# An attention stage whose tiles share a score bank, with two banks of turned tiles and probabilities scaled on GpSimd

## The chip, the cores and the metric

The kernel runs on one core of one Trainium2 chip. The metric is the device time of one execution in microseconds, the median of the runs. Engines are named as in the profile: PE (TensorE matmuls), PEld (its weight loads), DVE (VectorE), ACT (ScalarE), POOL (GpSimd), SP (SyncE).

## The reference

Two transformer layers over 256 context and 1024 latent tokens of width 1024: a gated linear attention layer, then a latent-attention (MLA) layer, each followed by a convolutional feed-forward. The change touches only the attention of the second layer, in fp32:

```
q = rmsnorm((rmsnorm(cq) @ w_uq) per head, q_norm)      # 8 heads, 128 + 64 rotary
k, v = (rmsnorm(ckv) @ w_ukv) per head                  # k_nope 128, v 128
k = rmsnorm(concat(k_nope, k_pe), k_norm)               # over 192
q, k = rope on the last 64
s = q @ k.T * 192 ** -0.5                               # 1024 x 1280 per head
o = softmax(s) @ v
```

## The kernel before

Every fp32 product is made of three passes over fp32r parts: high times high, high times low, low times high. A value is split by copying it to an fp32r tile (its high part, on ACT or POOL) and subtracting that from the original (its low part, on DVE or POOL).

The attention is one stage, with the instruction order of each engine written out by hand. A head has 8 tiles of 128 queries; a tile t has three units, so 24 units a head, numbered 3t + n. For each unit PE, in order: *turns* a part of the probabilities of tile t (`turn_p`, L1633: matmuls against the identity, keys onto partitions, written to PSUM), does any preparation piece due in this unit, then does the third n of the *scores* of tile t+2 (L1621, 12 matmuls of 512 columns and 6 of 256 for a tile). Before an even tile it multiplies the two turned tiles before it with v (`values`, L1644, 30 matmuls of 256 columns). So each engine works two tiles behind the scores.

The others follow: ACT copies the turned part to `pt_hi` (L1738), DVE subtracts to `pt_lo` (L1835). On ACT the exponential of tile t+1 (L1719, which also sums) stands behind the copy of n = 0. On DVE the row maximum of t+1 (L1809, L1814) stands ahead of the subtraction of n = 0; behind that of n = 1 stand the reciprocal of the sum (L1819) and the scaling of the probabilities of t+1 (L1821).

PSUM has 8 banks of 512 columns. Scores of even tiles start at bank 0, those of odd tiles at bank 3, 2.5 banks each; the output of `values` lies in the upper half of bank 2; turned parts have one bank (6), preparation one (7, `work`). With one bank for turned parts, `turn_p` of a unit waits for the subtraction of the unit before:

```
UNITS = ((0, 4), (4, 4), (8, 2))                      # first key tile, key tiles
S_PS, O_PS, T_PS, W_PS = (0, 3 * BANK), 2 * BANK + 256, 6 * BANK, 7 * BANK
pe.wait_ge(ptl_set, h * (QT * NU) + (t * NU + n + 1)) # in turn_p
```

The next head's keys and queries are made in *pieces* between the units, by the table PREPARE: k in three parts with their squares (POOL, L1540), the sums of squares over partitions (k_sum), log and exp for the reciprocal root (ACT, k_log, k_rstd), k_norm (DVE, L1784), the rotary part of k (POOL, L1544, L1547), the high part of k (POOL, L1551), k_low (DVE, L1788), and for each half of the queries q, q_pe (12 matmuls of 512 columns, L1588; q_turn on DVE, L1799), q_pe_low (L1804), q_sum (L1594, 4 products with one column each; two instructions each in the trace, whose squares POOL adds, L1559). All pieces go through the one bank `work`, so each waits for the reader of the one before. The v pieces of the head itself (L1599) are made in units 1 to 3. The head's weights are loaded by SP when all pieces of the head before are done, and split on POOL.

Head 0 is prepared ahead of the loop over the heads, with no tiles beside it. Heads 1 to 6 are a hardware loop of two heads a turn, heads 0 and 7 stand outside it.

Of the kernel before, what the change touches and what calls it, by code (L numbers as in the profile page):

```python
# [26 lines left out]
ALU = mybir.AluOpType  # L27
# [1312 lines left out]
def mla_latents(c, a, raw, cq_hi, cq_lo, ckv, ckv_hi, ckv_lo, k_pe, pe_sq, rope, norms, half):  # L1340
# [16 lines left out]
    with c.stage() as block:  # L1357
# [65 lines left out]
        def _(pool):  # L1423
# [8 lines left out]
PREPARE = {5: (("k", 0),), 7: (("k", 1),), 8: (("k", 2),), 9: (("k_sum", 0),), 10: (("k_sum", 1),),  # L1432
           11: (("k_sum", 2),), 12: (("k_log", 0),), 13: (("k_rstd", 0), ("q", 0)),
           14: (("k_norm", 0), ("q_pe", 0)), 15: (("k_low", 1), ("q_pe_low", 0)), 16: (("k_low", 0), ("q_sum", 0)),
           19: (("q", 1),), 20: (("q_pe", 1),), 21: (("q_pe_low", 1),), 22: (("q_sum", 1),)}

PIECES = (("k", 0), ("k", 1), ("k", 2), ("k_sum", 0), ("k_sum", 1), ("k_sum", 2), ("q", 0), ("q_pe", 0),
          ("q_sum", 0), ("q", 1), ("q_pe", 1), ("q_sum", 1), ("v", 0), ("v", 1), ("v", 2))
# [4 lines left out]
def attention(c, a, cq_hi, cq_lo, ckv, ckv_hi, ckv_lo, k_pe, pe_sq, rope, norms, o2):  # L1443
# [21 lines left out]
    q_sq = c.at("q_sq", 176, [P, 2, BANK])  # L1465
    wkv = c.at("wukv", 206, [P, 2 * P])
# [8 lines left out]
    q_eps = c.at("q_eps", 20.5, [P, 1])  # L1475
    (wkv_in, wq_in, w_hi_set, w_split, consts_set, piece_done, act_read, dve_read, k_sq_set, k_logged,
     k_rstd_set, k_normed, kp_set, k_hi_set, k_lo_set, q_sq_set, q_added, q_hi_set, q_pe_hi_set, q_lo_set,
     q_rstd_set, v_hi_set) = c.sems(
        "wkv_in", "wq_in", "w_hi_set", "w_split", "consts_set", "piece_done", "act_read", "dve_read", "k_sq_set",
# [5 lines left out]
    UNITS = ((0, 4), (4, 4), (8, 2))  # L1485
# [4 lines left out]
    S_PS, O_PS, T_PS, W_PS = (0, 3 * BANK), 2 * BANK + 256, 6 * BANK, 7 * BANK  # L1490
# [4 lines left out]

    def begins(h):
        return isinstance(h, int) and h == 0

# [8 lines left out]
    with c.stage() as block:  # L1507
        @block.sync
        def _(sp):
            sp.dma_start(wkv[:, :], a["wukv"][0]).then_inc(wkv_in, 16)  # L1510
            sp.dma_start(wq[:, :, :], a["wuq"][0]).then_inc(wq_in, 16)
            with sp.Fori(0, MH - 1, 1) as h:
                sp.wait_ge(piece_done, h * NP + NP)
                sp.wait_ge(w_split, h * 2 + 2)
                sp.dma_start(wkv[:, :], a["wukv"][h + 1]).then_inc(wkv_in, 16)
                sp.dma_start(wq[:, :, :], a["wuq"][h + 1]).then_inc(wq_in, 16)

        @block.gpsimd
        def _(pool):

            with pool.Fori(0, MH // 2, 1) as i:
                for slot in range(2):
                    h = i * 2 + slot
                    pool.wait_ge(wkv_in, (h + 1) * 16)
                    pool.nop(nofuse=True)
                    pool.tensor_scalar(wk_hi[:, :], wkv[:, 0:P], 1.0, 1.0, ALU.mult, ALU.mult
                                       ).then_inc(w_hi_set, 1)
                    pool.wait_ge(w_hi_set, h * 2 + 1)
                    pool.tensor_tensor(wk_lo[:, :], wkv[:, 0:P], wk_hi[:, :].bitcast(F32), ALU.subtract
                                       ).then_inc(w_split, 1)  # L1530
                    pool.wait_ge(wq_in, (h + 1) * 16)
                    pool.nop(nofuse=True)
                    pool.tensor_scalar(wq_hi[:, :, :], wq[:, :, :], 1.0, 1.0, ALU.mult, ALU.mult
                                       ).then_inc(w_hi_set, 1)
                    pool.wait_ge(w_hi_set, h * 2 + 2)
                    pool.tensor_tensor(wq_lo[:, :, :], wq[:, :, :], wq_hi[:, :, :].bitcast(F32),
                                       ALU.subtract).then_inc(w_split, 1)
                    for g, (t, m) in enumerate(KEYS):
                        pool.wait_ge(act_read, h * NA + (g + 1))
                        pool.tensor_tensor(sq[:, t:t + m], kf[:, t:t + m], kf[:, t:t + m], ALU.mult  # L1540
                                           ).then_inc(k_sq_set, 1)
                    pool.wait_ge(k_rstd_set, h + 1)
                    pool.wait_ge(k_lo_set, h * 2 + 1)
                    pool.tensor_tensor(kp[:, :], k_pe[:, :], rstd[:, :], ALU.mult).then_inc(kp_set, 1)  # L1544
                    pool.wait_ge(kp_set, h + 1)
                    pool.nop(nofuse=True)
                    pool.tensor_scalar(k_hi[:, slot, 1, :], kp[:, :], 1.0, 1.0, ALU.mult, ALU.mult  # L1547
                                       ).then_inc(k_hi_set, 1)
                    pool.wait_ge(k_normed, h + 1)
                    pool.nop(nofuse=True)  # L1550
                    pool.tensor_scalar(k_hi[:, slot, 0, :], kf[:, :], 1.0, 1.0, ALU.mult, ALU.mult  # L1551
                                       ).then_inc(k_hi_set, 1)
                    for part in range(2):
                        pool.wait_ge(dve_read, h * NV + (5 + 2 * part))
                        pool.nop(nofuse=True)
                        pool.tensor_scalar(q_hi[:, 1, part * BANK:(part + 1) * BANK], q_turn[:, :], 1.0, 1.0,
                                           ALU.mult, ALU.mult).then_inc(q_pe_hi_set, 1)
                        pool.wait_ge(q_sq_set, h * 4 + (2 * part + 2))
                        pool.tensor_tensor(q_sq[0:ROPE, 0, :], q_sq[0:ROPE, 0, :], q_sq[0:ROPE, 1, :],  # L1559
                                           ALU.add).then_inc(q_added, 1)  # L1560

        @block.tensor
        def _(pe):
            def piece(h, step, part, slot):
# [26 lines left out]
                elif step == "q_sum":  # L1591
                    pe.wait_ge(q_added, h * 2 + (part + 1))
                    for t in range(4):
                        mm = pe.matmul(work[:, t:t + 1], q_sq[:, 0, t * P:(t + 1) * P], c.ones[:, 0:1],  # L1594
                                       start=True, stop=True)
                else:
                    k0, w = UNITS[part]
                    for k in range(w):
                        mm = pe.matmul(work[:, k * P:(k + 1) * P], ckv[:, (k0 + k) * P:(k0 + k + 1) * P],  # L1599
                                       wkv[:, P:2 * P], start=True, stop=True)  # L1600
                mm.then_inc(piece_done, 1)

            def scores(h, t, g, slot):
# [8 lines left out]
                if g == 2 and t % 2 == 0:  # L1612

                    if t or not begins(h):
                        pe.wait_ge(o_set, h * PAIRS + t // 2)
                k0, w = KEYS[g]
                at = S_PS[t % 2] + k0
# [9 lines left out]
            def turn_p(h, t, n):  # L1627
                k0, w = UNITS[n]
                if n == 0:
                    pe.wait_ge(normed, h * QT + (t + 1))  # L1630
                pe.wait_ge(ptl_set, h * (QT * NU) + (t * NU + n + 1))
                for k in range(w):
                    mm = pe.transpose(c.psf[:, T_PS + k * P:T_PS + (k + 1) * P],  # L1633
                                      p[:, t % 2, (k0 + k) * P:(k0 + k + 1) * P], c.ident[:, :])
                mm.then_inc(turned, 1)

            def values(h, pair):
                pe.wait_ge(ptl_set, h * (QT * NU) + ((pair + 1) * 2 * NU + 1))
# [3 lines left out]
                for k in range(NT):  # L1642
                    for vv, pp in split_passes(v_hi, v_lo, pt_hi, pt_lo):
                        mm = pe.matmul(c.psf[:, O_PS:O_PS + 2 * P], vv[:, k, :], pp[:, k, :],  # L1644
                                       start=(k == 0 and vv is v_hi and pp is pt_hi),
                                       stop=(k == NT - 1 and vv is v_lo))
# [35 lines left out]
        def _(act):  # L1682
# [3 lines left out]
            def prepare(h, step, part):  # L1686
# [3 lines left out]
                if step == "k":  # L1690
                    if part == 0:
                        act.wait_ge(k_lo_set, h * 2 + 1)
                    t, m = KEYS[part]
# [8 lines left out]
                elif step == "q":  # L1702
                    act.activation(q_sq[:, 0, :], work, ACT.Square).then_inc(q_sq_set, 1)
                    act.activation(q_hi[:, 0, half], work, ACT.Copy).then_inc(q_hi_set, 1)
                elif step == "q_pe":
                    act.activation(q_sq[:, 1, :], work, ACT.Square).then_inc(q_sq_set, 1)
# [21 lines left out]
            def body(h, slot, follows):  # L1728
                for t in range(QT):
                    for n, (k0, w) in enumerate(UNITS):  # L1730
                        unit = t * NU + n
                        act.wait_ge(turned, h * (QT * NU) + (t * NU + n + 1))
                        if t % 2 == 0 and n == 0:
                            if t:
                                out(h, t // 2 - 1)
                            elif not begins(h):
                                out(h - 1, PAIRS - 1)
                        act.activation(pt_hi[:, k0:k0 + w, t % 2 * P:t % 2 * P + P],  # L1738
                                       c.psf[:, T_PS:T_PS + w * P].rearrange("p (k t) -> p k t", t=P),
# [27 lines left out]
        def _(dve):  # L1767
# [5 lines left out]
            def prepare(h, step, part, slot):  # L1773
# [8 lines left out]
                elif step == "k_norm":  # L1782
                    dve.wait_ge(k_rstd_set, h + 1)
                    dve.scalar_tensor_tensor(kf[:, :], kf[:, :], k_weight[:, :], rstd[:, :], ALU.mult, ALU.mult  # L1784
                                             ).then_inc(k_normed, 1)
# [9 lines left out]
                elif step == "q_pe":  # L1795
                    dve.wait_ge(q_sq_set, h * 4 + (2 * part + 2))
# [20 lines left out]
            def normal(h, t):  # L1817
                dve.wait_ge(p_set, h * QT + (t + 1))
                dve.reciprocal(stats[:, INV, t:t + 1], stats[:, SUM, t:t + 1]).then_inc(inv_set, 1)  # L1819
                dve.wait_ge(inv_set, h * QT + (t + 1))  # L1820
                dve.tensor_scalar(p[:, t % 2, :], p[:, t % 2, :], stats[:, INV, t:t + 1], None, ALU.mult  # L1821
                                  ).then_inc(normed, 1)

            def body(h, slot, follows):
                for t in range(QT):
                    for n, (k0, w) in enumerate(UNITS):
                        unit = t * NU + n
                        at = slice(t % 2 * P, t % 2 * P + P)
                        if n == 0:
                            if t + 1 < QT:  # L1830
                                largest(h, t + 1)
                            elif follows:
# [3 lines left out]
                                          c.psf[:, T_PS:T_PS + w * P].rearrange("p (k t) -> p k t", t=P),  # L1836
# [212 lines left out]
```

## Time and profile before

| | us |
|---|---|
| median of 3 runs | 3782.52 (3782.37 to 3783.78) |
| profiled execution, its own time | 3785.08 |
| its span | 3783.3 |
| attention, first turning of head 0 to the last product | 2255.07 to 2909.6 |
| mean granted TensorE clock | 0.946 |

The profile is one execution; its own time lies 1.8 us above its span and 2.6 us above the median. Start times in it are from the start of the span. A matmul's duration holds its way through the array, so matmuls in a row start closer than they last: 0.23 us apart for 512 columns, 0.12 for 256. The granted clock is 1.0 for 2.4 GHz and 0.5 for 1.2 GHz.

### The profile page before, as it was taken

To read this page: it belongs to the slowest core of one execution; us is meant where nothing else is said; L and a number is where in the kernel's file an instruction comes from. 1 tells how busy PE (TensorE), PEld (TensorE's weight loads), DVE (VectorE), ACT (ScalarE), POOL (GpSimd) and SP (SyncE) were. 2 spreads that over 40 slices of the span, in tenths; PEclk is the share of its full clock that TensorE was granted. 3 is DMA by queue.
4 is the path that set the end of the run, shared out by engine and by line. 5 is a ranking of instruction groups with operands and counts; after the bars stand their busy time and mean duration, and the time that the engine had idled before them with its cause. 6 is when DMAs were issued, how large, how long until landed. Compare 5 with 4: busy or idle time off the path is not lost. (4 is left out here: it accounts for less than half of the span.)

```text
span 3783.3 us, 48952 instructions
## 1 busy us (share of the span) xinstructions
PE 3330.3 (88%) x17622; PEld 2791.9 (74%) x17622; DVE 2408.6 (64%) x2957; ACT 976.4 (26%) x1347; POOL 1033.0 (27%) x539
## 2 busy tenths in 40 slices
PE   2989958888789999999998668888886989999998
PEld 1879947777668888888886547767775768888886
DVE  7956079999736666666666346556565266666666
ACT  4011123333413111111111424444343131111111
POOL 0322135555122222222220122122121243333331
PEclk7999979999899999999999879999998989999999
DMA  5538120000411111110100100000001021111111
GB/s 202 181 132 277 57 84 1 0 0 0 146 40 40 39 33 42 35 39 33 44 33 4 67 14 5 5 5 5 5 5 61 31 67 48 50 45 47 46 50 56
DMA packets 62996, 196.29 MB, mean 52 GB/s; under 512 B 7536, under 2 KB 19696, under 8 KB 61488
## 3 DMA queue, kind: packets, MB, share of 16 engines
q1 hardware_dynamic: 46048, 164.35, 12.7%
q10 hardware_dynamic: 16848, 30.56, 2.3%
q8 instruction: 68, 1.11, 0.1%
q14 instruction: 32, 0.26, 0.0%
HBM read 176.02 MB, written 18.87 MB: 52 GB/s over the span
## 5 line engine op out<-in xcount | busy, mean ns | idle before, releaser
L1235 DVE SCALAR_TENSOR_TENSOR resid<-ps,mod,resid 128x512 f32<-128x512 f32 (+1 forms) x880 | 602.1, 697 | 470.8 <-PE ps L1131 469.6
L1138 PE MATMUL ps<-hf_hi,up_hi 128*128 128x512 f32 (+1 forms) x1760 | 652.9, 371 | 30.8 <-DVE hf_lo L283 21.8
L1138 PE MATMUL ps<-hf_lo,up_hi 128*128 128x512 f32 (+1 forms) x1760 | 652.6, 371 | 0.0
L1138 PE MATMUL ps<-hf_hi,up_lo 128*128 128x512 f32 (+1 forms) x1760 | 650.8, 370 | 0.0
L1106 POOL TENSOR_SCALAR up_hi<-up_raw 128x1024 fp32r<-128x1024 f32 x88 | 94.7, 1076 | 1161.3 <-PE ps L1138 1099.8
L1138 PEld LDWEIGHTS ps<-hf_hi,up_hi 128*128 128x128 f32 x1760 | 335.0, 190 | 87.5 <-issue 34.3
L1138 PEld LDWEIGHTS ps<-hf_hi,up_lo 128*128 128x128 f32 x1760 | 334.3, 190 | 56.4
L1138 PEld LDWEIGHTS ps<-hf_lo,up_hi 128*128 128x128 f32 x1760 | 335.0, 190 | 51.5
L1131 PE MATMUL ps<-act_hi,dn_hi 128*128 128x512 f32 (+1 forms) x880 | 333.5, 379 | 17.7 <-DVE act_lo L1256 16.1
L1131 PE MATMUL ps<-act_lo,dn_hi 128*128 128x512 f32 (+1 forms) x880 | 326.4, 371 | 0.0
L1131 PE MATMUL ps<-act_hi,dn_lo 128*128 128x512 f32 (+1 forms) x880 | 325.7, 370 | 0.0
L1187 ACT ACTIVATE conv<-ps,conv_w 128x1280 f32<-128x1280 f32 (+1 forms) x88 | 115.7, 1315 | 802.7 <-PE ps L1138 802.4
L667 POOL TENSOR_TENSOR k_decayed<-decay,qk 128x1280 f32<-128x1280 f32 x80 | 233.7, 2922 | 227.7 <-ACT decay L793 206.1
L126 DVE CUSTOM_DVE_ANT_0 ps<-adaw_ring,cond,adab 128x1024 f32<-128x1024 f32 x128 | 211.6, 1653 | 84.2 <-DMA adaw_ring<-in_adaw 74.1
L1835 DVE TENSOR_TENSOR pt_lo<-ps,pt_hi 128x512 fp32r<-128x512 f32 (+1 forms) x192 | 115.0, 599 | 220.7 <-ACT pt_hi L1738 220.2
L1131 PEld LDWEIGHTS ps<-act_hi,dn_hi 128*128 128x128 f32 x880 | 166.4, 189 | 71.1 <-DVE resid L1235 21.0
L1109 POOL TENSOR_TENSOR up_lo<-up_raw,up_hi 128x1024 fp32r<-128x1024 f32 x88 | 213.1, 2422 | 7.3
L561 PE MATMUL ps<-wvr_hi,h_hi 128*128 128x256 f32 x640 | 182.0, 284 | 16.2 <-POOL wvr_lo L547 16.2
L707 PE MATMUL ps<-q_decayed,k_decayed 128*128 128x128 f32 x1120 | 144.1, 281 | 59.0 <-DVE masked L875 57.6
L707 PEld LDWEIGHTS ps<-q_decayed,k_decayed 128*128 128x128 f32 x1120 | 133.9, 193 | 83.0 <-issue 82.1
L1131 PEld LDWEIGHTS ps<-act_lo,dn_hi 128*128 128x128 f32 x880 | 166.9, 190 | 28.5
L1131 PEld LDWEIGHTS ps<-act_hi,dn_lo 128*128 128x128 f32 x880 | 166.4, 189 | 28.8
(221 smaller groups left out, 7046.8 us busy)
## 6 DMA issues: line engine op xcount, KB each, us to landing
up_raw<-in_up SPq DMA_DIRECT2D x88, 512.0 KB, 3.3
adaw_ring<-in_adaw SPq DMA_DIRECT2D x80, 512.0 KB, 4.4
dn_raw<-in_dn SPq DMA_DIRECT2D x44, 512.0 KB, 3.2
vr<-vr_out ACTq DMA_DIRECT2D x80, 128.0 KB, 2.3
adaw_first<-in_adaw SPq DMA_DIRECT2D x16, 512.0 KB, 22.0
wvr_raw<-in_wvr SPq DMA_DIRECT2D x8, 1024.0 KB, 7.7
x<-in_xT ACTq DMA_DIRECT2D x8, 640.0 KB, 16.9
v<-vr SPq DMA_DIRECT2D x1, 5120.0 KB, 20.4
```

The source lines that it names most:

```text
L126: return dve.tensor_tensor_reduce(junk, w, self.cond[:, j, :], 1.0, self.bias[:, n:n + 1], ALU.mult, ALU.add, self.c.mod[:, n, j:j + 1])
L561: mm = pe.matmul(c.ps[:, u % RING, 0:W], a[:, k, t * P:(t + 1) * P], b[:, s, k, :], start=(k == 0 and a is h_hi and b is w_hi), stop=(k == ...
L667: pool.tensor_tensor(kd[u % 2][:, :].rearrange("p (b t) -> p b t", t=P), e[:, u % 2, :].rearrange("p (b t) -> p b t", t=P), qk[:, GH + h, ...
L707: pe.matmul(c.psf[:, TREE_PS + b * P:TREE_PS + (b + 1) * P], kd[u % 2][:, b * P:(b + 1) * P], qd[:, u % 2, b * P:(b + 1) * P], start=True, ...
L1106: pool.tensor_scalar(up_hi[:, half, :, :], up_raw[:, half, :, :], 1.0, 1.0, ALU.mult, ALU.mult).then_inc(up_hi_set, 1)
L1109: pool.tensor_tensor(up_lo[:, half, :, :], up_raw[:, half, :, :], up_hi[:, half, :, :].bitcast(F32), ALU.subtract).then_inc(up_split, 1)
L1131: mm = pe.matmul(c.ps[:, 6 + j % 2, 0:w], a[:, s, m * P:(m + 1) * P], b[:, s, t:t + w], start=(a is dn_hi and b is act_hi), stop=(a is dn_lo))
L1138: mm = pe.matmul(c.psf[:, at:at + w], a[:, half, k, :], b[:, k, t:t + w], start=(k == 0 and a is up_hi and b is h_hi), stop=(k == KD - 1 a ...
L1187: act.activation(y[:, half, span], u(half), ACT.Identity, scale=cw[:, bass.ds(f * 8 + (half * 4 + 1), 1)], bias=cw[:, bass.ds(f * 8 + (hal ...
L1235: dve.scalar_tensor_tensor(resid[:, m, t:t + w], c.ps[:, 6 + j % 2, 0:w], c.mod[:, gate + m, cond[t]:cond[t] + 1], resid[:, m, t:t + w], A ...
L1835: dve.tensor_tensor(pt_lo[:, k0:k0 + w, at], c.psf[:, T_PS:T_PS + w * P].rearrange("p (k t) -> p k t", t=P), pt_hi[:, k0:k0 + w, at].bitca ...
```

## The change

- Score bank: even tiles have columns 0 to 1279 of PSUM, odd ones 1280 to 2559, so both use a half of bank 2. An odd tile's keys are laid round by 256 columns (`column`), so that each third stays in a bank. The last third of the scores of a tile now waits for the exponential of the tile before it.
- Turned tiles: units are 4, 2 and 4 key tiles wide; those of n = 1 go to the lower half of bank 5 (the output of `values` lies in its upper half), those of n = 0 and 2 to bank 6. `turn_p` of n = 0 waits for the unit just before, n = 1 for three units back (and the output copy), n = 2 for two back. `values` starts without the last unit and waits for it ahead of key tile 6.
- The scaling of the probabilities moves from DVE to POOL. The reciprocal stays on DVE.
- Weights are loaded a head ahead; wukv is two loads, v's part with two slots. They are split on POOL in unit 0.
- k_norm is three instructions, one for each third of the keys, two in unit 14 and one in unit 15.
- q_sq gets a second buffer (over k_full), so the piece q(1) goes ahead of q_sum(0).
- Order: k pieces in units 4, 6, 8; q(0) 13; q_pe(0) 15 (was 14); q_pe_low(0) and k_low(0) 17; q(1) 18 (was 19); q_sum(0) 19 (was 16); q_pe(1) 20; q_sum(1) 23 (was 22). POOL's work follows the same table, with the scaling ahead of the pieces of its unit.

```diff
-PREPARE = {5: (("k", 0),), 7: (("k", 1),), 8: (("k", 2),), 9: (("k_sum", 0),), 10: (("k_sum", 1),),
-           11: (("k_sum", 2),), 12: (("k_log", 0),), 13: (("k_rstd", 0), ("q", 0)),
-           14: (("k_norm", 0), ("q_pe", 0)), 15: (("k_low", 1), ("q_pe_low", 0)), 16: (("k_low", 0), ("q_sum", 0)),
-           19: (("q", 1),), 20: (("q_pe", 1),), 21: (("q_pe_low", 1),), 22: (("q_sum", 1),)}
+PREPARE = {0: (("w", 0),), 4: (("k", 0),), 6: (("k", 1),), 8: (("k", 2),), 9: (("k_sum", 0),),
+           10: (("k_sum", 1),), 11: (("k_sum", 2),), 12: (("k_log", 0),), 13: (("k_rstd", 0), ("q", 0)),
+           14: (("k_norm", 0), ("k_norm", 1)), 15: (("k_norm", 2), ("q_pe", 0)), 16: (("k_low", 1),),
+           17: (("k_low", 0), ("q_pe_low", 0)), 18: (("q", 1),), 19: (("q_sum", 0),), 20: (("q_pe", 1),),
+           21: (("q_pe_low", 1),), 23: (("q_sum", 1),)}
...
-    UNITS = ((0, 4), (4, 4), (8, 2))
+    UNITS = ((0, 4), (4, 2), (6, 4))
...
-    S_PS, O_PS, T_PS, W_PS = (0, 3 * BANK), 2 * BANK + 256, 6 * BANK, 7 * BANK
+    S_PS, O_PS, W_PS = (0, T), 5 * BANK + 256, 7 * BANK
+    T_PS = (6 * BANK, 5 * BANK, 6 * BANK)
+    T_BEHIND = (1, 3, 2)
...
+            def normal(h, t):                                   # on POOL
+                pool.wait_ge(inv_set, h * QT + (t + 1))
+                pool.nop(nofuse=True)
+                pool.tensor_scalar(p[:, t % 2, :], p[:, t % 2, :], stats[:, INV, t:t + 1], None, ALU.mult
+                                   ).then_inc(normed, 1)
...
-                if g == 2 and t % 2 == 0:
-                    if t or not begins(h):
-                        pe.wait_ge(o_set, h * PAIRS + t // 2)
+                if g == 2 and (t or not begins(h)):
+                    pe.wait_ge(p_set, h * QT + t)
...
-                pe.wait_ge(ptl_set, h * (QT * NU) + (t * NU + n + 1))
+                if n == 1 and t % 2 == 0 and (t or not begins(h)):
+                    pe.wait_ge(o_set, h * PAIRS + (t // 2 + 1))
+                if not begins(h) or t * NU + n >= T_BEHIND[n]:
+                    pe.wait_ge(ptl_set, h * (QT * NU) + (t * NU + n + 2 - T_BEHIND[n]))
...
-                pe.wait_ge(ptl_set, h * (QT * NU) + ((pair + 1) * 2 * NU + 1))
+                pe.wait_ge(ptl_set, h * (QT * NU) + (pair + 1) * 2 * NU)
...
                 for k in range(NT):
+                    if k == UNITS[-1][0]:
+                        pe.wait_ge(ptl_set, h * (QT * NU) + ((pair + 1) * 2 * NU + 1))
...
-                dve.wait_ge(inv_set, h * QT + (t + 1))
-                dve.tensor_scalar(p[:, t % 2, :], p[:, t % 2, :], stats[:, INV, t:t + 1], None, ALU.mult
-                                  ).then_inc(normed, 1)
```

## Rows read from the trace of the kernel before

**Rows 1.** The page: span, and busy time of each engine.
```profile
span 3783.3 us, 48952 instructions
PE 3330.3 (88%) x17622; PEld 2791.9 (74%) x17622; DVE 2408.6 (64%) x2957; ACT 976.4 (26%) x1347; POOL 1033.0 (27%) x539
```

**Rows 2.** Stretches of heads 2 and 7: length, each engine's busy time, clock, DMA.
```profile
2420.01:2508.03 88.02, 73.21 (x421) 61.30 (x420) 49.45 (x71) 34.47 (x62) 17.49 (x14) 0.92 0.02 6
...
2843.31:2909.60 66.29, 54.43 (x330) 44.12 (x328) 32.00 (x53) 25.40 (x46) 0.00 (x0) 0.92 0.00 0
```

**Rows 3.** Waits, 2254 to 2905: who waited for whom: us, times, longest.
```profile
PEld ps L1633 <- DVE pt_lo L1835: 76.5, 77, 2.1
...
PE ps L1633 <- DVE pt_lo L1835: 45.0, 66, 1.7
```

**Rows 4.** Timeline (start, us, engine, line): turnings opening units 0, 6, 12, 18, 0.
```profile
2337.19 0.60 PE L1633 MATMUL ps<-ident,p 128*128 128x128 f32 x4
...
2355.28 0.60 PE L1633 MATMUL ps<-ident,p 128*128 128x128 f32 x4
...
2373.18 0.60 PE L1633 MATMUL ps<-ident,p 128*128 128x128 f32 x4
...
2399.07 0.60 PE L1633 MATMUL ps<-ident,p 128*128 128x128 f32 x4
...
2420.01 0.60 PE L1633 MATMUL ps<-ident,p 128*128 128x128 f32 x4
```

**Rows 5.** Timeline of a pair without pieces, tiles 4 and 5 of head 7.
```profile
2876.09 0.60 PE L1633 MATMUL ps<-ident,p 128*128 128x128 f32 x4
...
2879.07 0.60 ACT L1738 ACTIVATE pt_hi<-ps 128x512 fp32r<-128x512 f32 x1
...
2881.91 0.63 PE L1633 MATMUL ps<-ident,p 128*128 128x128 f32 x4 [0.32 <-DVE pt_lo L1835]
...
2891.29 0.60 PE L1633 MATMUL ps<-ident,p 128*128 128x128 f32 x4
```

**Rows 6.** Groups by line and shape, 2254 to 2905: busy us, mean ns.
```profile
L1809 DVE TENSOR_REDUCE stats<-ps 128x1 f32<-128x1280 f32 x63 | 93.6, 1486 | 7.5 <-PE ps L1621 7.0
L1835 DVE TENSOR_TENSOR pt_lo<-ps,pt_hi 128x512 fp32r<-128x512 f32 x128 | 88.1, 688 | 195.3 <-ACT pt_hi L1738 194.8
L1821 DVE TENSOR_SCALAR p<-p,stats 128x1280 f32<-128x1280 f32 x64 | 63.6, 994 | 2.3
...
L1784 DVE SCALAR_TENSOR_TENSOR k_full<-k_full,k_weight,rstd 128x1280 f32<-128x1280 f32 x7 | 19.2, 2739 | 0.0
...
L1719 ACT ACTIVATE p<-ps,stats 128x1280 f32<-128x1280 f32 x63 | 89.5, 1421 | 36.2 <-DVE stats L1814 36.2
...
L1697 ACT ACTIVATE rstd<-rstd,eps 128x1280 f32<-128x1280 f32 x7 | 9.6, 1372 | 0.0
...
L1544 POOL TENSOR_TENSOR k_pe_full<-k_pe,rstd 128x1280 f32<-128x1280 f32 x7 | 22.8, 3256 | 119.4 <-ACT rstd L1701 119.4
L1547 POOL TENSOR_SCALAR k_hi<-k_pe_full 128x1280 fp32r<-128x1280 f32 x7 | 16.2, 2321 | 1.1 <-POOL k_pe_full L1544 1.1
...
L1551 POOL TENSOR_SCALAR k_hi<-k_full 128x1280 fp32r<-128x1280 f32 x7 | 8.8, 1263 | 0.0
```

**Rows 7.** Timeline of head 1, units 14 to 17, at the pieces of q.
```profile
2380.91 0.50 PE L1588 MATMUL ps<-cq_hi,wuq_hi 128*128 128x512 f32 x1 [1.64 <-DVE q_lo L1793]
...
2386.74 2.53 POOL L1559 TENSOR_TENSOR q_sq<-q_sq 64x512 f32<-64x512 f32 x1
2386.80 0.65 PE L1633 MATMUL ps<-ident,p 128*128 128x128 f32 x4 [1.70 <-DVE pt_lo L1835]
...
2389.41 1.84 PE L1594 MATMUL ps<-ones,q_sq 128*128 128x1 f32 x8 [1.95 <-POOL q_sq L1559]
...
2391.68 0.63 PE L1621 MATMUL ps<-k_lo,q_hi 128*128 128x512 f32 x1
2392.11 0.63 PE L1621 MATMUL ps<-k_hi,q_lo 128*128 128x512 f32 x1
```

## What the change will do, predicted before it was run

> **What bounds the kernel now.** I read the page first. Over the whole span PE is busy 88% [rows 1], but that is a mean over stages; the change touches one stage of 654.5 us (2255.07 to 2909.6), so I cut that into heads. In one of 88 us PE is busy 73, DVE 49, ACT 34, POOL 17.5 [rows 2]: no engine but PE is near full, and PE has holes. The waits say whose: most are `turn_p` waiting for `pt_lo` (76.5 us on its weight loads, 45.0 on its matmuls) [rows 3]. An idle time on PE costs more than it reads, since matmuls in a row overlap. So I use starts: the distance between two turnings holds all that PE did and waited for between.
>
> The four pairs of tiles of head 1 take 18.1, 17.9, 25.9 and 20.9 us [rows 4]. A pair with no pieces, in head 7, takes 15.2 [rows 5]. What does PE need for it? Per tile twelve 512-wide score matmuls (2 x 1.48 us, the first of a block starting some 0.1 late), six 256-wide ones (0.79), ten turnings (0.86), and 30 x 0.12 = 3.6 for `values`: 2 x 4.61 + 3.6 = 12.8. So 2.4 us of a plain pair are waits. The four pairs of a head need 51.3, its pieces (v 2.0, k 1.8, k_sum 2.2, q 5.6, q_sum 1.7) some 13: 64.5 of 82.8. The other 18 are what the change can reach. The third pair, 25.9 us, is the worst [rows 7]: q_pe waits 1.64 us for q_lo in `work`; k_norm, one DVE instruction of 2.74 us [rows 6], stands ahead of the row maximum and makes the turning wait 1.70; q_sum waits 1.95 for squares; and behind these holes the scores start 0.43 us apart in place of 0.23, the 1.2 GHz level.
>
> **The change part by part.** I lay the instructions of each engine out for a pair, with the trace's durations and 0.05 us from engine to engine (0.15 to and from POOL, as from 2386.74 + 2.53 to 2389.41 [rows 7]).
>
> *A plain pair.* With two banks, turnings stand at 0, 1.84 (1.48 of scores behind 0.36) and 3.46, with no wait. ACT copies unit 1 at 2.98 as before, since that stands behind the exponential (2879.07 - 2876.09 [rows 5]). It is 256 wide now, so copy and subtraction take 0.39 + 0.42; the reciprocal ends at 3.90. Then POOL scales. No row shows POOL scaling by a value per partition. The nearest by shape and kind is its 1280-wide TENSOR_SCALAR (L1551), 1.26 us; the same operation beside a busy DVE (L1547) takes 2.32, and the slowest 1280-wide POOL operation, 3.26 [rows 6]. I take 1.26, because DVE then reads PSUM; from below DVE's own 0.99 bounds it (L1821 [rows 6]). So tile o may be turned at 3.90 + 0.15 + 1.26 + 0.15 = 5.47. The other condition, unit 2's subtraction (turned 4.06, copy 0.60, subtraction 0.69), gives 5.45: a tie. Before, 5.82 [rows 5]. From there nothing waits: 5.47 + 4.61 + 3.6 = 13.7, against 15.2: **1.5 us a pair**. The new wait of the last third of scores for an exponential costs nothing: the exponential of the pair's second tile is over at about 3.0, the block comes at 3.8; in the second tile 8.5 against 9.2. That is the thinnest cover, 0.7 us. The output copy ahead of unit 1 is over by 1.1, cover 0.7.
>
> *Units 0 to 5, with v.* v pieces fill PE. The row maximum of tile 2 starts behind the subtraction of unit 2 at 6.6, so its exponential runs from 8.3 to 9.8; only then ACT copies v(2), DVE subtracts until 11.1, and k(0), now in unit 4, not 5, waits for that from 9.3: 1.9 us. Result 18.1, before 18.1. No gain.
>
> *Units 6 to 11.* The scaling of tile 3 stands on POOL behind the squares of k(1) (1.04), so the turning comes at 6.3 and not 5.8; then PE goes through: 16.8, before 17.9. Gain 1.1.
>
> *Units 12 to 17.* Counted from the turning of unit 12. q_pe, a unit later, no longer waits for q_lo. But ACT has a list ahead of the copy of unit 14: exponential to 3.0 (1.42), k_log to 4.3 (1.37 [rows 6]), copy of unit 13, k_rstd (as k_log) to 5.8, q's square and copy (0.6 each) to 6.8, then the copy to 7.2 and the subtraction to 8.1. PE is through with unit 14 at 6.0 and turns unit 15 at 8.1. Two k_norm parts (2.74 x 512/1280 = 1.1 each [rows 6]) come first on DVE, so the row maximum of tile 6 runs from 10.2 to 11.7 and the exponential to 13.5; scores(7,2) wait 0.1. q's square on ACT, q_turn on DVE (as the 0.69 of a subtraction) and the subtraction of unit 16 make `values` start at 15.2 in place of 14.3; k_low (about the 1.49 of the row maximum, also 1280 wide [rows 6]) stands ahead of the subtraction of unit 17, which holds the last 12 matmuls to 17.7: end at 19.1. On POOL the scaling of tile 6 stands behind k_hi, q_hi and the addition of squares (2.53 when k_low runs beside it [rows 7]) and then shares time with the second k_low: over at 20.4. So unit 18 opens at 20.5, before 25.9: gain 5.4, of which 0.8 is q_sum moving out, the rest the k_norm, q_pe and q_sum waits and the clock behind them.
>
> *Units 18 to 23.* q(1) sits in `work` until ACT has done the exponential of tile 7 (to 3.9 from the turning of unit 18, its row maximum standing behind k_low and q_pe_low) and two copies (4.9), and DVE has subtracted (5.7); PE is there at 3.9: q_sum(0) waits 1.8 us. Otherwise PE goes through: 19.8, before 20.9, with 0.8 more work.
>
> *Sum of a head*: 18.1 + 16.8 + 20.5 + 19.8 = 75.2, against 82.8. This is at full clock. Two low stretches a head stay likely in weaker form (q_sum behind its 1.8 wait, unit 15); the last pair, 20.9 here, is 1.1 above its least, so I add 1.2 a head. Heads 2 and 4 have 5.2 us more than their neighbours, at the jump back of the loop [rows 2]; it stays. So seven heads (588.2 us): 7 x (75.2 + 1.2) + 2 x 5.2 = 545.2, gain 43.0.
>
> *Head 7* (66.3 [rows 2]) has no pieces: 2.0 in the first pair (without k(0)'s wait), 1.5 and 1.5, and some 4.3 in the last, where nothing but turnings is left and each waited a full copy and subtraction: 9.3.
>
> *Head 0's preparation*: k_low no longer stands between q's halves, q(1) ahead of q_sum(0) saves its round, about 3; the first scaling on POOL adds 0.7: gain 2.3.
>
> *At nothing*: loads and split of the weights (POOL has 57 idle us of a head [rows 2]; 3.1 us of splitting in unit 0 are over before tile 1 must be scaled at 4.8; without that cover, 3.1 once a head). DVE freed of 64 x 0.99 = 63.6 us: no bound of its own, its gain is in the pairs.
>
> Total 43.0 + 9.3 + 2.3 = 54.6. The profiled execution's 3785.1 becomes 3730.5; the median lies 2.6 below that: **3728**.
>
> One rule of the Trainium skill speaks against the change. GPSIMD Engine Reference, § 8 Key points, calls VectorE "structurally ~2× faster" for elementwise work. Taken so, the scaling would be 2 x 0.99 = 1.98 us and the second tile's turning 0.7 later in each of 32 pairs, 23 us, or 3751; its § 4.1 calls one-input work roughly line rate, which row L1551 bears out, so I keep 1.26.
>
> **The rivals.**
> - *POOL is slow in the scaling* (as L1547, 2.32 us [rows 6]): each pair's second tile waits 1.06 more, 32 x 1.06 = 34: 3762. For it: POOL's rows do swell beside DVE. Against: at that point DVE reads PSUM, and L1551 next to such work stays at 1.26.
> - *Slower than before, by the same place*: the pair loses all it won when the scaling takes 1.26 + 54.6/32 = 2.97. At L1544's 3.26 [rows 6] it is 64 us: 3728 + 64 = 3792. For it: the operand is new for POOL. Against: L1544 has two tensor inputs, the scaling one.
> - *The clock stays as low as before*: at 0.43 in place of 0.23 [rows 7], head 1 has about 2.9 us of it in the third pair and 1.1 in the last, with 1.2 allowed; 7 x 3 = 21: 3749. For it: q_sum's one-column products behind a wait are what preceded it [rows 7]. Against: three waits of 1.6 to 1.95 in a row become one.
> - *The waits only move*: the single `work` bank and ACT's fixed order give back what the banks win; plain pairs tie at 5.45 already. Heads stay at 82: 3778 to 3785.
> - *Better*: if the waits before unit 15 and q_sum(0) (2.1 and 1.8) do not come, 7 x 3.9 = 27: 3701.
>
> **How the numbers follow.** Forecast as summed (3712 to 3742) 0.55; clock as before 0.12; slow POOL 0.08; better 0.11; waits only move 0.06; slower 0.08. For the time to fall within 8 in 10 the range runs from 3704 (most of the better case) to 3764 (through the clock and the slow POOL). 0.2% is 7.6 us, about what a measurement can tell from no change. Faster by that: 0.55 + 0.12 + 0.08 + 0.11 = 0.86; within it 0.06; slower 0.08.
>
> **What would show it.** Head 7's pairs at 13.7; POOL's scaling row at 1.26; the heads at 76, the jump-back ones at 81; turnings' waits for `pt_lo` nearly gone, and in their place a wait for POOL at the second tile of a pair; q_sum(0) behind q_lo, k(0) behind v_lo; fewer 0.43-spaced matmuls. It would be wrong if POOL's row is over 2 us, if the last third of scores waits for an exponential (cover 0.7), or if the third pair stays above 23.

## The result and the profile after

The changed kernel takes 3810.78 us (median of 4 runs, 3804.65 to 3813.65), beside 3783.15 for the kernel before on the same chip: a ratio of 1.0069 (1.0052 to 1.0087). It is slower by 0.7%, where 3728 and faster was forecast. The page of its profile, with the columns of [rows 1], and the one row of its costliest groups that is new:

```profile
span 3811.0 us, 49150 instructions
...
PE 3330.5 (87%) x17622; PEld 2809.6 (74%) x17622; DVE 2376.1 (62%) x2909; ACT 967.4 (25%) x1347; POOL 1247.0 (33%) x603
...
L1588 POOL TENSOR_SCALAR p<-p,stats 128x1280 f32<-128x1280 f32 x64 | 225.2, 3519 | 270.2 <-DVE stats L1881 270.2
```

PE does the same work in the same busy time. POOL has 214 us more. The new group, the 64 scalings, makes 225 us, 3.52 us each; the rest of POOL's work is 11 us shorter. The prediction had them at 1.26. The waits from 2254 to 2930 (who, for whom; us, times, longest):

```profile
PE ps L1686 <- POOL p L1588: 84.8, 33, 4.5
...
PEld ps L1686 <- POOL p L1588: 41.4, 15, 4.7
PEld ps L1686 <- issue: 34.7, 26, 2.7
...
PEld ps L1686 <- DVE pt_lo L1894: 20.6, 8, 3.0
```

The turnings' waits for `pt_lo`, 76.5 and 45.0 us in [rows 3], have fallen to 20.6 on the weight loads and 1.8 on the matmuls. A wait for POOL stands in their place. Heads 2 and 7 as stretches, with the columns of [rows 2]:

```profile
2427.22:2520.25 93.03, 74.38 (x421) 64.19 (x420) 45.96 (x65) 33.25 (x62) 46.23 (x25) 0.89 0.02 6
2866.82:2937.00 70.18, 55.42 (x330) 48.70 (x328) 26.14 (x46) 24.60 (x46) 24.63 (x7) 0.85 0.00 1
```

Both are longer (88.02 and 66.29 in [rows 2]), and the clock is lower: 0.89 and 0.85 in place of 0.92. The turnings that open the pairs of head 1, as in [rows 4]:

```profile
2341.79 0.60 PE L1686 MATMUL ps<-ident,p 128*128 128x128 f32 x4
...
2361.67 0.60 PE L1686 MATMUL ps<-ident,p 128*128 128x128 f32 x4
...
2380.38 0.60 PE L1686 MATMUL ps<-ident,p 128*128 128x128 f32 x4
...
2403.90 0.66 PE L1686 MATMUL ps<-ident,p 128*128 128x128 f32 x4 [2.35 <-POOL p L1588]
...
2427.22 0.60 PE L1686 MATMUL ps<-ident,p 128*128 128x128 f32 x4
```

The pairs take 19.9, 18.7, 23.5 and 23.3 us; 18.1, 17.9, 25.9 and 20.9 before [rows 4]. Only the third is shorter. It is still above 23, which the prediction had named as a sign that it would be wrong. The mechanism is plainest in a pair without pieces, tiles 2 and 3 of head 7, which stands for [rows 5]:

```profile
2884.22 0.60 PE L1686 MATMUL ps<-ident,p 128*128 128x128 f32 x4
...
2887.78 0.15 DVE L1881 RECIPROCAL stats<-stats 128x1 f32<-128x1 f32 x1
...
2888.10 3.52 POOL L1588 TENSOR_SCALAR p<-p,stats 128x1280 f32<-128x1280 f32 x1 [5.01 <-DVE stats L1881]
...
2891.67 1.12 PE L1686 MATMUL ps<-ident,p 128*128 128x128 f32 x4 [2.70 <-POOL p L1588]
2892.44 0.78 PE L1670 MATMUL ps<-k_hi,q_hi 128*128 128x512 f32 x1
...
2893.01 0.63 PE L1670 MATMUL ps<-k_lo,q_hi 128*128 128x512 f32 x1
...
2893.44 0.63 PE L1670 MATMUL ps<-k_hi,q_lo 128*128 128x512 f32 x1
...
2902.72 0.60 PE L1686 MATMUL ps<-ident,p 128*128 128x128 f32 x4
```

Everything up to the reciprocal is as laid out: it ends at 3.71 from the opening (3.90 forecast). The scaling then lasts 3.52, and PE, idle for 2.70, turns the second tile at 7.45 (5.47 forecast, 5.82 before). Behind that idle time the scores start 0.43 us apart, the level of 1.2 GHz. The granted clock says the same (stretch: length, each engine's busy time, clock, DMA), here from the turning to the end of the slow matmuls and behind them:

```profile
2891.67:2897.70 6.03, 6.03 (x17) 4.87 (x18) 1.19 (x3) 2.38 (x4) 0.81 (x1) 0.50 0.00 0
2897.90:2902.70 4.80, 4.80 (x42) 4.72 (x40) 2.30 (x3) 0.60 (x1) 2.51 (x1) 1.00 0.02 3
```

The pair takes 18.5, the next 17.3; 13.7 was forecast for each, 15.2 measured before.

### The profile page after: what moved, and what is told of

Same layout as the page of the kernel before. It is cut to its first block and busy times, and to the rows that moved or that the text cites. A ratio compares the mean times of both kernels' runs of the same rounds, so it can differ in the third digit from the quotient of the medians.

```text
span 3811.0 us, 49150 instructions
## 1 busy us (share of the span) xinstructions
PE 3330.5 (87%) x17622; PEld 2809.6 (74%) x17622; DVE 2376.1 (62%) x2909; ACT 967.4 (25%) x1347; POOL 1247.0 (33%) x603
## 5 line engine op out<-in xcount | busy, mean ns | idle before, releaser
L1588 POOL TENSOR_SCALAR p<-p,stats 128x1280 f32<-128x1280 f32 x64 | 225.2, 3519 | 270.2 <-DVE stats L1881 270.2
L561 PE MATMUL ps<-wvr_hi,h_hi 128*128 128x256 f32 x640 | 182.1, 284 | 16.3 <-POOL wvr_lo L547 16.3
L1686 PE MATMUL ps<-ident,p 128*128 128x128 f32 x640 | 112.6, 294 | 87.0 <-POOL p L1588 84.8
```

The source lines that it names most:

```text
L561: mm = pe.matmul(c.ps[:, u % RING, 0:W], a[:, k, t * P:(t + 1) * P], b[:, s, k, :], start=(k == 0 and a is h_hi and b is w_hi), stop=(k == ...
L1588: pool.tensor_scalar(p[:, t % 2, :], p[:, t % 2, :], stats[:, INV, t:t + 1], None, ALU.mult).then_inc(normed, 1)
L1686: mm = pe.transpose(c.psf[:, T_PS[n] + k * P:T_PS[n] + (k + 1) * P], p[:, t % 2, at:at + P], c.ident[:, :])
```

## The experiments

Each run has its own median of the kernel before beside it (3778.9 to 3783.2 us), so ratios compare runs better than microseconds do.

**Theory A**: POOL's scaling, at 3.5 us, takes the place of the wait that the banks removed; the rest does what was forecast. Within it, A1: POOL is slow because the operand is one value per partition; A2: because of something else in the instruction. **Theory B**: the new order of pieces and the tighter banks lose the time.

### The scaling back on DVE (e1_scale_on_dve)

```diff
-            def normal(h, t):                                   # POOL
...
+                dve.wait_ge(inv_set, h * QT + (t + 1))          # behind the reciprocal, as before
+                dve.tensor_scalar(p[:, t % 2, :], p[:, t % 2, :], stats[:, INV, t:t + 1], None, ALU.mult
+                                  ).then_inc(normed, 1)
```

> The changed kernel with one part undone: the probabilities are scaled by DVE again, right behind the reciprocal; all else as changed. Theory A (the whole loss is POOL's scaling, 3.52 us a tile where 1.26 was taken): the scaling is 0.89 to 0.99 us again, the turning of a pair's second tile comes at about 5.5 us, a pair without pieces takes 13.7 to 14.0 us, a head about 76, and the kernel comes out near the sum of the prediction, 3728 (ratio 0.981 to 0.990). Theory B (the waits only move: the work bank and the fixed orders give back what the banks win): heads of 80 us and more, 3765 to 3785, ratio 0.995 to 1.001.

Measured: 3738.64 us, 0.9891 (0.9875 to 0.9908). Pairs of head 1: 18.1, 16.7, 21.6, 19.4, against 18.1, 16.8, 20.5, 19.8 forecast. This is within the range of Theory A (0.981 to 0.990). All that is lost hangs on where and how the scaling is done; B falls as the cause of the loss.

### The scaling alone on POOL (e2_before_pool_scale)

The kernel before, with its one bank and its order; POOL's work follows the units, as its program must once the scaling stands in it.

```diff
+PREPARE = {4: (("w", 0),), 5: (("k", 0),), ...
...
+                pool.tensor_scalar(p[:, t % 2, :], p[:, t % 2, :], stats[:, INV, t:t + 1], None, ALU.mult
+                                   ).then_inc(normed, 1)
...
-                dve.tensor_scalar(p[:, t % 2, :], p[:, t % 2, :], stats[:, INV, t:t + 1], None, ALU.mult
-                                  ).then_inc(normed, 1)
```

> The kernel before with one part done alone: the scaling moves to POOL (its program follows the units, with the scaling ahead of a unit's pieces). Theory A: at 3.52 us plus two hand-overs the second tile of a pair is turned about 2.4 us later (3.9 + 0.4 + 3.8 = 8.2 in place of 5.8), the first tile is covered by values: 32 x 2.4 = 77, less what pieces cover, 3840 to 3860, ratio 1.013 to 1.020. Theory B (POOL's scaling is mostly hidden, the rest of the change costs): under 3795, ratio under 1.004.

Measured: 3877.45, 1.0268 (1.0251 to 1.0286); the scaling 3.64 us each. That is more than Theory A gave (1.013 to 1.020). The same edit costs the kernel before 98 us, and the new one 72 (3810.8 against 3738.6; 67 by the ratios); e13 below parts the 98.

### The banks alone (e4_banks_alone)

The kernel before with the three edits of the score bank, the turned tiles' banks and `values`.

```diff
-    UNITS = ((0, 4), (4, 4), (8, 2))
+    UNITS = ((0, 4), (4, 2), (6, 4))
...
+    S_PS, O_PS, W_PS = (0, T), 5 * BANK + 256, 7 * BANK
+    T_PS = (6 * BANK, 5 * BANK, 6 * BANK)
+    T_BEHIND = (1, 3, 2)
```

> The kernel before with the PSUM part alone: shared score bank, two banks of turned tiles, units of 4, 2 and 4, values starting ahead of the last unit. Scaling on DVE, pieces, weights and order as before. If the banks give what was worked out for a plain pair (1.5 us), head 7 falls by 8 to 9 and the others by 3 to 5 each: 3740 to 3755, ratio 0.989 to 0.993. If the pieces' waits take it back: 3775 to 3785, ratio 0.998 to 1.001.

Measured: 3730.28, 0.9879 (0.986 to 0.9898), a little better than the 0.989 to 0.993 expected. The banks alone give as much as everything but the POOL scaling together (e1, 0.9891). In head 7's pair without pieces the second tile is turned at 5.55, with DVE scaling in 0.89 us. The shared score bank, the second bank of turned tiles and the earlier `values` were not tried one by one.

### What makes POOL slow (e3, e7, e6)

Three kernels change the operands of the one instruction. e3_pool_constants and e7_pool_constant_one_op leave out the scaling of the probabilities (they multiply by 1); e6_pool_operand_two_ops multiplies by the reciprocal and then by 1, so it computes the same as the changed kernel. Below, `p..` stands for `p[:, t % 2, :]`.

```diff
-pool.tensor_scalar(p.., p.., stats[:, INV, t:t + 1], None, ALU.mult)
+pool.tensor_scalar(p.., p.., 1.0, 1.0, ALU.mult, ALU.mult)                    # e3
+pool.tensor_scalar(p.., p.., 1.0, None, ALU.mult)                             # e7
+pool.tensor_scalar(p.., p.., stats[:, INV, t:t + 1], 1.0, ALU.mult, ALU.mult) # e6
```

> The changed kernel with POOL's scaling taking two constants of 1.0 in place of the value per partition: same tile, same place, same waits, so the probabilities stay unscaled. Theory A1 (the operand per partition makes POOL slow): the row falls from 3.52 to about 1.26 us, and the kernel to 3725 to 3745. Rival A2 (POOL is slow there through the place: in place on p, or DVE beside it): the row stays at 3.5 us and the time at 3805 to 3815.

> The changed kernel; POOL's scaling takes one constant of 1.0 and no second operation (the probabilities stay unscaled). If the operand per partition is the cost, the row is 1.26 to 1.4 us and the time 3735 to 3745. If the form with one operation is, it stays at about 3.5 us and 3805 to 3815.

> The changed kernel; POOL's scaling keeps its operand per partition and gets a second operation with a constant 1.0. If the operand per partition is what makes it 3.5 us, the row stays at 3.4 us or more. If it is the form with one operation, it falls to about 1.3 to 1.4 and the time to 3735 to 3745.

Measured: 3741.15 (0.9901, 0.9884 to 0.9917), 3800.95 and 3741.97 us (one run each for the last two). Their groups of the scaling (busy us, mean ns, idle before), first e3:

```profile
L1588 POOL TENSOR_SCALAR p<-p 128x1280 f32<-128x1280 f32 x64 | 89.6, 1400 | 294.4 <-DVE stats L1881 294.4
```

e7, constant, one operation:

```profile
L1588 POOL TENSOR_SCALAR p<-p 128x1280 f32<-128x1280 f32 x64 | 220.6, 3447 | 271.3 <-DVE stats L1881 271.3
```

e6, value per partition, two operations:

```profile
L1588 POOL TENSOR_SCALAR p<-p,stats 128x1280 f32<-128x1280 f32 x64 | 98.1, 1533 | 289.6 <-DVE stats L1881 289.6
```

The operand makes 0.07 to 0.13 us, the number of operations 2.0: with one, 3.45 and 3.52 us; with two, 1.40 and 1.53. e3 alone had come out as A1 said (1.40 us, 3741), but it changes the operand and the number of operations together; e6 and e7 part the two, and A1 falls. The instruction that does less work on paper is the slow one. Why it is slow no run shows.

### Two operations, timed (e10_pool_two_ops)

> The changed kernel with one argument of POOL's scaling changed: the value per partition stays the first operand, and a second operation multiplies by a constant 1.0 (as e6_pool_operand_two_ops, now timed). Theory C, formed after e6 and e7: the form with a single operation is what makes POOL's 1280-wide scaling 3.5 us; with two it is 1.4 to 1.5, and the kernel is 3738 to 3746, ratio 0.988 to 0.992. If the single look was chance: above 0.995.

The edit is e6's. Measured: 3737.77, 0.9889 (0.9874 to 0.9904), level with e1. A plain pair of head 7:

```profile
2822.63 0.60 PE L1686 MATMUL ps<-ident,p 128*128 128x128 f32 x4
...
2826.18 0.15 DVE L1881 RECIPROCAL stats<-stats 128x1 f32<-128x1 f32 x1
...
2826.50 1.33 POOL L1588 TENSOR_SCALAR p<-p,stats 128x1280 f32<-128x1280 f32 x1 [6.48 <-DVE stats L1881]
...
2828.18 0.63 PE L1686 MATMUL ps<-ident,p 128*128 128x128 f32 x4 [0.80 <-DVE pt_lo L1894]
...
2836.38 0.60 PE L1686 MATMUL ps<-ident,p 128*128 128x128 f32 x4
```

The scaling is over at 5.20 of the pair, the second tile is turned at 5.55, and the wait before it is for `pt_lo`, not for POOL: the tie that the prediction found between the two conditions (5.47 and 5.45). The pair takes 13.75, at a granted clock of 1.00 throughout. And the pairs of head 1:

```profile
2327.31 0.60 PE L1686 MATMUL ps<-ident,p 128*128 128x128 f32 x4
...
2345.38 0.60 PE L1686 MATMUL ps<-ident,p 128*128 128x128 f32 x4
...
2362.07 0.60 PE L1686 MATMUL ps<-ident,p 128*128 128x128 f32 x4
...
2384.67 0.66 PE L1686 MATMUL ps<-ident,p 128*128 128x128 f32 x4 [1.95 <-POOL p L1588]
...
2405.18 0.60 PE L1686 MATMUL ps<-ident,p 128*128 128x128 f32 x4
```

18.07, 16.69, 22.60 and 20.51 us, where 18.1, 16.8, 20.5 and 19.8 were forecast.

### The scaling alone, with two operations (e13_before_pool_two_ops)

e2 with e6's instruction.

> e2_before_pool_scale with the form of two operations: the kernel before, scaling on POOL. Theory C: of the 2.7% that e2 lost nearly all comes back; 3.9 + 0.3 + 1.45 = 5.65 at the second tile against 5.8 of the kernel before, so 3780 to 3800, ratio 0.999 to 1.005. If POOL is the wrong engine in any form: above 1.01.

Measured: 3805.93, 1.0075 (1.0061 to 1.0089), the scaling at 1.46 us; 0.999 to 1.005 was expected. So the one operation costs 71.5 us here (3877.45 - 3805.93), about what it costs the changed kernel, whatever the banks (73 us by the medians, 3810.78 - 3737.77, and 68 by the ratios); the other 26 are a second loss. The first pair of a head takes 3.4 us more than before on average, 24 in seven heads (the other pairs of those heads together are 7 us shorter). Unit 5 of head 1 shows why:

```profile
2354.94 1.33 POOL L1567 TENSOR_SCALAR p<-p,stats 128x1280 f32<-128x1280 f32 x1 [5.91 <-DVE stats L1845]
...
2356.24 0.30 POOL L1525 TENSOR_SCALAR wuk_hi<-wukv 128x128 fp32r<-128x128 f32 x1
...
2356.62 0.45 POOL L1528 TENSOR_TENSOR wuk_lo<-wukv,wuk_hi 128x128 fp32r<-128x128 f32 x1
...
2357.13 0.70 PE L1604 MATMUL ps<-ckv_hi,wuk_hi 128*128 128x512 f32 x1 [1.94 <-POOL wuk_lo L1528]
```

The split of the next head's weights stands behind the scaling on POOL, and PE, which needs them at once for k(0), waits 1.94, and as long or a little longer in each of the seven heads. The other 1.5 is the clock behind that wait: it is 0.92 over this pair and 1.00 over the same pair before, and in the one head whose pair keeps 1.00 the pair is only 2.2 longer. In the changed kernel the weights are split in unit 0 and this wait does not occur: the edit that the prediction put at nothing is of use once the scaling is on POOL.

### The order of the pieces (e5, e9, e11)

e5_k0_later is e1 with k(0) in unit 5, as before. e9_order is e5 with q_sum(0) in unit 18, ahead of q(1). e11_order_pool_two_ops is e9 with e6's scaling on POOL.

```diff
-PREPARE = {0: (("w", 0),), 4: (("k", 0),), 6: (("k", 1),), ...   18: (("q", 1),), 19: (("q_sum", 0),), ...
+PREPARE = {0: (("w", 0),), 5: (("k", 0),), 6: (("k", 1),), ...   18: (("q", 1),), 19: (("q_sum", 0),), ... # e5
+PREPARE = {0: (("w", 0),), 5: (("k", 0),), 6: (("k", 1),), ...   18: (("q_sum", 0),), 19: (("q", 1),), ... # e9
```

> The kernel with DVE scaling (e1_scale_on_dve) and one step of the order put back: the first piece of k in unit 5 again, not 4. In e1_scale_on_dve units 4 and 5 take 4.22 + 4.74 us; if k(0) waits in unit 4 for DVE's subtraction of the last v piece (1.9 us in the prediction), they become 1.6 + 5.6 and a head is 1.7 us shorter: 12 us less than e1_scale_on_dve, ratio to before 0.984 to 0.988. If the wait only moves to unit 5 or 6: no change from e1_scale_on_dve, 0.988 to 0.991.

> As e5_k0_later, and q_sum(0) goes ahead of q(1) again, in unit 18, q(1) in unit 19. In e1_scale_on_dve units 18 and 19 take 3.19 + 4.63, of which 1.6 to 1.8 is q_sum(0) waiting for q_lo behind the exponential; ahead of q(1) it should find its squares added: 2.7 + 3.0. So 2.1 us a head less than e5_k0_later, 27 less than e1_scale_on_dve: ratio to before 0.979 to 0.984. The rival: q(1) in unit 19 pushes q_pe(1) in unit 20 into a wait for q_lo of the same size, and the ratio is that of e5_k0_later.

> e9_order with the scaling on POOL in the form with two operations. If DVE's time matters once POOL's form is mended, it beats e9_order: ratio 0.980 to 0.984. If not, since POOL's scaling is 0.5 us longer, stands behind other POOL work and holds up k_low, it is the same or a little slower: 0.985 to 0.990. The second is the likelier, as e1_scale_on_dve and e3_pool_constants were alike.

Measured: e5 3726.07 (0.9853, 0.9838 to 0.9868), e9 3724.1 (0.9854, 0.9838 to 0.9871), e11 3730.68 (0.9869, 0.9853 to 0.9885). In e1 the wait that e5 removes, at the first k matmul:

```profile
2263.79 0.50 PE L1614 MATMUL ps<-ckv_hi,wuk_hi 128*128 128x512 f32 x1 [1.52 <-DVE v_lo L1894]
```

(That is head 0; in the other heads it is 1.66.) The first pair falls from 18.1 to 16.3, and the kernel by 12.6 us = 7 x 1.8, and the two intervals do not meet. In e5 q_sum(0) of head 1 waits as forecast (1.8 to 1.9 in three heads, 0.5 to 0.7 in the other four):

```profile
2386.48 1.05 PE L1631 MATMUL ps<-ones,q_sq 128*128 128x1 f32 x8 [1.86 <-DVE q_lo L1844]
```

In e9 it does not, but q(1) then waits 0.70 for the reader of q_sum(0), and the whole gives 2 us, less than a measurement can tell; 0.979 to 0.984 was expected, and the rival, the ratio of e5, came true. e11 came out as its likelier case.

### k_norm in one instruction (e12_k_norm_whole)

e5 with k_norm whole, in unit 14.

```diff
-           14: (("k_norm", 0), ("k_norm", 1)), 15: (("k_norm", 2), ("q_pe", 0)), 16: (("k_low", 1),),
+           14: (("k_norm", 2),), 15: (("q_pe", 0),), 16: (("k_low", 1),),
```

> e5_k0_later with k_norm as one DVE instruction in unit 14 again. If the three parts are worth something, units 14 to 17 grow, since the row maximum of tile 6 comes later by the third part (0.5 us): 0.5 us a head, 3 to 4 in all, ratio 0.986 to 0.988. If the whole instruction brings back the 1.7 us wait of the kernel before: 8 to 12 us, ratio 0.988 to 0.990. If nothing depends on it: 0.985 to 0.986, as e5_k0_later.

Measured: 3718.31, 0.9837 (0.9823 to 0.9851), the fastest of all and faster than any of the three cases expected; the interval overlaps e5's. The group of e12:

```profile
L1835 DVE SCALAR_TENSOR_TENSOR k_full<-k_full,k_weight,rstd 128x1280 f32<-128x1280 f32 x7 | 15.2, 2178 | 0.0
```

and the two of e5:

```profile
L1835 DVE SCALAR_TENSOR_TENSOR k_full<-k_full,k_weight,rstd 128x512 f32<-128x512 f32 x14 | 21.3, 1557 | 0.0
...
L1835 DVE SCALAR_TENSOR_TENSOR k_full<-k_full,k_weight,rstd 128x256 f32<-128x256 f32 x7 | 3.3, 475 | 0.0
```

Three parts cost 2 x 1.56 + 0.48 = 3.6 us, the whole 2.2. The first two alone, which stand ahead of the row maximum, are 3.1. The third pair of head 1 takes 20.8 in place of e5's 21.6.

## Why the prediction was wrong

**The step that failed** is one term: "Then POOL scales ... I take 1.26". It measured 3.52, and the prediction's own sign, a row over 2 us, came true. The row it was taken from (L1551 [rows 6]) has the same shape and opcode, but two operations; the scaling has one. That could be read in the source: every TENSOR_SCALAR of POOL in the kernel before is written `1.0, 1.0, mult, mult`, and the diff has `None` in the second place. With two operations the scaling is 1.33 us in the plain pair and 1.53 on average (e6, e10), so the choice among the rows was sound for a form that the kernel did not use. By the prediction's own rule the price would be (3.52 - 1.26) x 32 pairs = 72, 3728 + 72 = 3800. Measured between the forms: 3810.8 - 3737.8 = 73, or 68 by the ratios. That 72 comes so near is partly luck, since the loss is made up otherwise (below). Of the rivals, the slower one had the place right and gave 3792; its threshold, 2.97 us, was passed, but no run lies between 1.53 and 3.45 to test it. The ground it was turned down on, that L1544 has two tensor inputs and the scaling one, said nothing on an instruction that no row of before showed. The thought that DVE reads PSUM meanwhile said as little: e7 and e3 differ by 2.0 us beside the same DVE work. One reading is off without consequence: the 57 idle us of POOL are those of the forecast head (75.2 - 17.5); in [rows 2] it is 70.5.

The rule weighed there, "structurally ~2× faster" for VectorE (the Trainium skill, GPSIMD Engine Reference, § 8 Key points), fits neither form: against DVE's 0.99 us POOL takes 1.5 times as long with two operations and 3.5 times with one. Its § 4.1, one-input work at roughly line rate, is near the first and far off the second.

**How 3.5 us becomes more than its difference.** The second tile comes 1.90 later (7.45 against 5.55 in e10), but the plain pair is 4.75 longer (18.50 against 13.75). The other 2.85 is clock: behind the idle time the scores start 0.43 apart, not 0.23, at a granted clock of 0.50 where e10 has 1.00. In pairs with pieces PE fills part of the wait, and head 1's grow by 1.8, 2.0, 0.9 and 2.8 from e10. Up to the last product the changed kernel is 72.8 us longer than e10: 3.6 in the preparation of head 0, 56.2 in the 28 pairs of heads 0 to 6 (2.0 a pair) and 13.1 in the 4 of head 7 (3.3 a pair), where the sum had 2.26 in each.

A slow POOL also holds DVE. In the changed kernel, around unit 17 of head 2:

```profile
2483.23 2.51 POOL L1582 TENSOR_TENSOR q_sq<-q_sq 64x512 f32<-64x512 f32 x1
...
2485.13 5.01 DVE L1850 TENSOR_TENSOR k_lo<-k_full,k_hi 128x1280 fp32r<-128x1280 f32 x1
...
2485.73 3.51 POOL L1588 TENSOR_SCALAR p<-p,stats 128x1280 f32<-128x1280 f32 x1
...
2489.30 0.66 PE L1686 MATMUL ps<-ident,p 128*128 128x128 f32 x4 [2.35 <-POOL p L1588]
...
2495.77 1.86 PE L1642 MATMUL ps<-ones,q_sq 128*128 128x1 f32 x8 [2.85 <-DVE q_lo L1855]
```

and in e10, at the same place:

```profile
2458.65 2.02 DVE L1850 TENSOR_TENSOR k_lo<-k_full,k_hi 128x1280 fp32r<-128x1280 f32 x1
2459.26 3.12 POOL L1588 TENSOR_SCALAR p<-p,stats 128x1280 f32<-128x1280 f32 x1
...
2462.44 0.66 PE L1686 MATMUL ps<-ident,p 128*128 128x128 f32 x4 [1.96 <-POOL p L1588]
```

In the changed kernel k_low takes 5.01, its own 1.5 and the whole 3.51 of POOL's instruction. So it does in each of the seven heads prepared beside tiles; it is 1.48 with the scaling on DVE (e1) and before. PE waits twice behind the two, 2.35 for the scaling and 2.85 for q_lo. With two operations it is the other way round: k_low takes 2.02, and the scaling is the one that is stretched, to 3.12 from 1.33, and PE waits 1.96 for it. That DVE and GpSimd exclude each other when a DVE instruction has two inputs in SBUF is in the Trainium skill (SBUF — State Buffer, § Who interferes with whom), and the durations here agree. It also says that the one issued first goes first. These rows do not settle that: k_low starts 0.6 us ahead of the scaling in both kernels and is held by it in only one, and both times POOL was still in the instruction before, L1582, until the scaling began (2483.23 + 2.51 = 2485.74).

**What was right**, read from e10, where only that term is mended. Plain pair 13.75 (13.7). Units 0 to 5: 18.1, k(0)'s wait included (e5 takes it out: 1.8 a head, 1.9 forecast). Units 6 to 11: 16.7 (16.8). q_sum(0)'s wait is 1.33 in e10 and 1.86 with the scaling on DVE (e1; 1.8 forecast). The last third of the scores waits for an exponential once in all heads, 0.3 us. Head 7, from its opening to the last product: 56.4 against 65.6, a gain of 9.2 (9.3). That the waits for `pt_lo` go and a wait for POOL comes at the second tile is what the changed kernel's waits show. The third pair's clock came back, too: 1.00 in e10, 0.87 before.

**What was off beside it**: e10's span is 43.0 below that of before, not 54.6. By first turnings and last products, the preparation gives 4.1 (2.3 forecast), heads 0 to 6 give 32.1 (43.0), head 7 9.2, and 2.4 are lost behind it. The third pair is 22.6 and not 20.5: k_norm's parts were taken as 2.74 x 512/1280 = 1.1 each and are 1.90 there (1.56 with the scaling on DVE), and PE waits 1.95 at unit 18 for the scaling of tile 6, the one stretched to 3.12 beside k_low. With the scaling on DVE the pair is 21.6 (e1). The two heads at the jump back cost 7.2 and 5.4 more than their neighbours, not 5.2 each. The clock recovered in part only: over the attention it is 0.95 in e10 and 0.93 before; head 1's last pair stays at 0.92, and in e5 the scores behind q_sum(0)'s wait still start 0.43 apart. That these shares come from those causes is read from the rows; only k_norm's was tried by itself (e12, 7.8 us with overlapping intervals).

**Where the gain is.** The banks: 0.9879 alone. With k(0) and k_norm put back as they were, the other edits add 0.4% (e12, 0.9837, an interval apart from that of e4); which of them does, no run shows. The scaling on POOL takes 64 us of work from DVE and gives nothing: e10 and e1 are level, and e11 is 6.6 us above e9, with overlapping intervals. In a plain pair the second tile is turned at 5.55 with either engine (e4, e10), since both times it waits for unit 2's subtraction. The best version keeps the scaling on DVE, k(0) in unit 5 and k_norm whole: 3718.31 us, 1.6% under before.

## What to carry to other kernels

When work moves to another engine, price the exact instruction, with its number of operations and the kind of its operands; a row with the same opcode and shape was off by 2.8 times here (3.52 against 1.26). Where the range of a price spans the break-even of the whole change, the forecast is as uncertain as that price, and a chance of 0.08 for its far side looks low. The banks brought three quarters of the best version's gain (1.2% of 1.6%); two of the edits that came with them, k(0) a unit earlier and the scaling on POOL, cost or gave nothing, and k_norm in parts seems to have cost.

## What the runs showed of the hardware

- POOL's TENSOR_SCALAR on 128 x 1280 fp32 takes 3.45 to 3.64 us on average with one operation (after, e2, e7) and 1.40 to 1.53 with a second one that multiplies by 1.0 (e3, e6, e10, e13); a constant or a value per partition as the first operand makes 0.13 us at most.
- A DVE subtraction with two inputs in SBUF and a POOL scaling held each other up where they met: 5.01 and 3.51 us with the one-operation form (the subtraction alone lengthened), 2.02 and 3.12 with two operations (both lengthened). Elsewhere the subtraction takes 1.48, the scaling 3.52 and 1.33.
- k_norm on DVE takes 1.56 us for 512 columns and 2.18 for 1280 (e5, e12), so a part is not its share of the whole; in other company the same instructions take up to 2.18 and 3.45 (after, e13). The runs do not show how much of that is POOL beside it.
- After an idle 2.70 us, PE ran its next 4 turning matmuls in 1.12 us in place of 0.60 and its scores at the 1.2 GHz level; the granted clock was 0.50 for 6.0 us and 1.00 behind that.
